# A new order of the scan's operations on the five engines of a hybrid encoder kernel

## What is computed

```
def _wkv_step(S, xs):
    r_t, w_t, k_t, v_t, kk_t, a_t = xs
    sa = jnp.einsum('zbhvk,zbhk->zbhv', S, -kk_t)
    S = (S * w_t[..., None, :]
         + sa[..., :, None] * (kk_t * a_t)[..., None, :]
         + v_t[..., :, None] * k_t[..., None, :])
    o = jnp.einsum('zbhvk,zbhk->zbhv', S, r_t)
    return S, o
...
_, o = lax.scan(_wkv_step, S0, seqs)
```

## Time and profile before

| | us |
|---|---|
| median of 3 runs | 3039.69 (3038.88 to 3043.14) |
| profiled execution, its own time | 3045.98 |
| its span in the trace | 3044.2 |
| scan: unit 0's first matmuls to unit 24's `logits` | 938.00 to 1577.09 |
| scan: from there to the last store | 1577.09 to 1662.21 |
| PE busy in the span | 2655.3 (87%) |
| DVE, ACT, POOL busy | 1410.2, 801.5, 980.1 |

### The profile page before, as it was taken

One profiled execution on the slowest core, in us unless ns is written; L12 is line 12 of the kernel. 1 busy time (PEld: TensorE's weight loads), 2 busy tenths in 40 slices (PEclk: granted clock), 3 DMA queues, 4 the chain that ended last, 5 costly groups with the idle time before them and its releaser, 6 DMA issues. The chain is left out here.

```text
span 3044.2 us, 56483 instructions
## 1 busy us (share of the span) xinstructions
PE 2655.3 (87%) x23399; PEld 2286.7 (75%) x23399; DVE 1410.2 (46%) x2263; ACT 801.5 (26%) x1412; POOL 980.1 (32%) x604
## 2 busy tenths in 40 slices
PE   2599969599995888889986596999999999999996
PEld 1488858455554888888885375999999988999996
DVE  5335435455554565656652695332323263323235
ACT  2212111244442333333331221222122232212211
POOL 3215215346662121211210573332232333323221
PEclk9999989599996899999998698999999999999998
DMA  4222221100002111111111534422212213122211
GB/s 146 68 69 92 67 86 47 58 21 18 8 11 63 49 52 52 55 46 56 49 34 42 181 138 167 128 63 61 69 55 69 62 53 108 55 69 64 60 41 41
DMA packets 210810, 203.48 MB, mean 67 GB/s; under 512 B 16982, under 2 KB 174678, under 8 KB 210618
## 3 DMA queue, kind: packets, MB, share of 16 engines
q1 hardware_dynamic: 210618, 200.67, 21.5%
HBM read 153.45 MB, written 47.18 MB: 66 GB/s over the span
## 5 line engine op out<-in xcount | busy, mean ns | idle before, releaser
L2368 POOL TENSOR_TENSOR ff_w_lo<-ff_w,ff_w_hi 128x1024 fp32r<-128x1024 f32 x132 | 317.4, 2428 | 734.2 <-ACT ff_w_hi L2423 540.0
L2640 PE MATMUL ff_gu<-ff_x_hi,ff_w_hi 128*128 128x384 f32 x1408 | 473.4, 336 | 7.9 <-DVE ff_x_lo L2512 7.9
L2640 PE MATMUL ff_gu<-ff_x_hi,ff_w_lo 128*128 128x384 f32 x1408 | 472.6, 336 | 0.0
L2640 PE MATMUL ff_gu<-ff_x_lo,ff_w_hi 128*128 128x384 f32 x1408 | 472.5, 336 | 0.0
L2521 DVE SCALAR_TENSOR_TENSOR ff_th<-ff_th,ff_gu 128x384 f32<-128x384 f32 x88 | 48.8, 554 | 557.2 <-ACT ff_th L2435 557.2
L2640 PEld LDWEIGHTS ff_gu<-ff_x_hi,ff_w_hi 128*128 128x128 f32 x1408 | 266.0, 189 | 9.3 <-DVE ff_x_lo L2512 8.4
L2640 PEld LDWEIGHTS ff_gu<-ff_x_hi,ff_w_lo 128*128 128x128 f32 x1408 | 266.1, 189 | 0.9
L2640 PEld LDWEIGHTS ff_gu<-ff_x_lo,ff_w_hi 128*128 128x128 f32 x1408 | 265.9, 189 | 0.0
L2534 DVE TENSOR_TENSOR ff_y<-ff_dn,ff_y 128x512 f32<-128x512 f32 x264 | 179.1, 689 | 121.2 <-PE ff_dn L2651 121.0
L2651 PE MATMUL ff_dn<-ff_w_hi,ff_a_hi 128*128 128x512 f32 x528 | 207.1, 392 | 6.9 <-DVE ff_y L2534 6.8
L2651 PE MATMUL ff_dn<-ff_w_hi,ff_a_lo 128*128 128x512 f32 x528 | 206.8, 392 | 0.0
(11 more groups left out here) (273 smaller groups left out, 5269.1 us busy)
## 6 DMA issues: line engine op xcount, KB each, us to landing
ff_w<-in_w_ffn_in SPq DMA_DIRECT2D x88, 512.0 KB, 5.0
ff_w<-in_w_ffn_out SPq DMA_DIRECT2D x44, 512.0 KB, 3.7
sc_x<-scratch_chT SPq DMA_DIRECT2D x72, 256.0 KB, 3.3
pj_x<-in_x SPq DMA_DIRECT2D x13, 512.0 KB, 3.6
co_w<-in_w_in SPq DMA_DIRECT2D x13, 512.0 KB, 5.7
scratch_chT<-co_sh SPq DMA_DIRECT2D x8, 785.0 KB, 4.3
scratch_scan<-sc_out SPq DMA_DIRECT2D x24, 260.0 KB, 2.6
mo_sc<-scratch_scan SPq DMA_DIRECT2D x24, 260.0 KB, 3.0
```

The costliest lines, as they stand in the source:

```text
L2368: nc.gpsimd.tensor_tensor(w_lo[:, q, x, :], w[:, q, x, :], w_hi[:, q, x, :].bitcast(F32), ALU.subtract).then_inc(done, 1)
L2640: last = nc.tensor.matmul(gu[:, g, m, 0:GRP], ww[:, q, m, k * P:(k + 1) * P], xx[:, k, g * GRP:(g + 1) * GRP], start=(j == 0), stop=(j == ...
```

## The change

The three tables that give each operation its place are replaced by other numbers, and the three constants that spaced prep, level and back part (`LEAD`, `LEVEL_SPAN`, `BACK_AT`) are gone, since the new numbers hold the places themselves. No operation is added or removed, and no wait: each operation keeps the semaphores it had.

```
-LEVEL = (("x0", -0.17),) + tuple((f"{x}{l}", (l - 1 + at) / 5) for l in range(1, LEVELS) for x, at in (("y", 0.05), ("mask", 0.25), ("t", 0.5), ("add", 0.75)))
...
-LEAD, LEVEL_SPAN, BACK_AT = 1.4, 1.5, 1.6
...
+LEVEL = (("x0", -0.149), ("y1", -0.0), ("mask1", 0.16), ("t1", 0.221), ("add1", 0.28), ("y2", 0.431), ("mask2", 0.507), ("t2", 0.569), ("add2",
...
+REUSE_AT, VALUES_AT, STORE_AT = -0.73, 2.71, 2.76
...
-    stages = [(u - LEAD + at, 0, "prep", name, u) for u in range(UNITS) for name, at in PREP]
-    stages += [(u + at * LEVEL_SPAN, 1, "level", name, u) for u in range(UNITS) for name, at in LEVEL]
-    stages += [(u + BACK_AT + at, 2, "back", name, u) for u in range(1, UNITS) for name, at in BACK]
-    stages += [(BACK_AT, 3, "meta", "", 0)]
+    stages = [(u + at, 0, "prep", name, u) for u in range(UNITS) for name, at in PREP]
+    stages += [(u + at, 1, "level", name, u) for u in range(UNITS) for name, at in LEVEL]
+    stages += [(u + at, 2, "back", name, u) for u in range(1, UNITS) for name, at in BACK]
+    stages += [(dict(LEVEL)["add5"], 3, "meta", "", 0)]
```

More of the change, by code:

```diff
@@ L1241 @@
 HALF_DECAY = DECAY / 2
-PREP = (("logits", 0.0), ("tanhw", 0.02), ("eye", 0.05), ("tanha", 0.07), ("cum", 0.1), ("gate", 0.12), ("lift", 0.14),
[3 rows of a table removed]
-LEVEL = (("x0", -0.17),) + tuple((f"{x}{l}", (l - 1 + at) / 5) for l in range(1, LEVELS) for x, at in (("y", 0.05), ("mask", 0.25), ("t", 0.5), ("add", 0.75)))
-BACK = (("drive", 0.02), ("carry0", 0.05), ("U1_0", 0.1), ("solve0", 0.16), ("U0", 0.21), ("state0", 0.28), ("H0", 0.34),
-        ("carry1", 0.48), ("U1_1", 0.55), ("solve1", 0.61), ("U1", 0.66), ("state1", 0.73), ("H1", 0.79), ("emit", 0.87), ("out", 0.95))
+PREP = (("logits", -1.328), ("tanha", -1.264), ("tanhw", -1.241), ("gate", -1.218), ("lift", -1.179), ("kd", -1.128), ("cum", -1.112), ("rkd",
[3 rows of a table added]
+LEVEL = (("x0", -0.149), ("y1", -0.0), ("mask1", 0.16), ("t1", 0.221), ("add1", 0.28), ("y2", 0.431), ("mask2", 0.507), ("t2", 0.569), ("add2",
+         0.621), ("y3", 0.724), ("mask3", 0.776), ("t3", 0.936), ("add3", 0.988), ("y4", 1.049), ("mask4", 1.101), ("t4", 1.157), ("add4", 1.209),
+         ("y5", 1.312), ("mask5", 1.494), ("t5", 1.526), ("add5", 1.586))
+BACK = (("drive", 1.773), ("carry0", 1.855), ("U1_0", 1.904), ("solve0", 1.985), ("U0", 2.013), ("state0", 2.098), ("H0", 2.13), ("carry1", 2.273),
+        ("U1_1", 2.322), ("solve1", 2.361), ("U1", 2.389), ("state1", 2.621), ("emit", 2.647), ("out", 2.691), ("H1", 2.798))
 RING = 4
-LEAD, LEVEL_SPAN, BACK_AT = 1.4, 1.5, 1.6
+REUSE_AT, VALUES_AT, STORE_AT = -0.73, 2.71, 2.76
 UNITS = 2 * STEPS + 1
@@ L1470, in store @@
                     sp.dma_start(d["scan"][un.s, un.tile * P:(un.tile + 1) * P, :], out[:, un.ring, :]).then_inc(out_stored[un.ring], 16)
-                moves = [(un.u - 2 - LEAD + 0.47, load, un) for un in units[1:]]
-                moves += [(un.u - RING + BACK_AT + 1, load_values, un) for un in units[1:]]
-                moves += [(un.u + BACK_AT + 1, store, un) for un in units[1:]]
+                moves = [(un.u - 2 + REUSE_AT, load, un) for un in units[1:]]
+                moves += [(un.u - RING + VALUES_AT, load_values, un) for un in units[1:]]
+                moves += [(un.u + STORE_AT, store, un) for un in units[1:]]
                 for _, move, un in sorted(moves, key=lambda x: x[0]):
```

## The result

The changed kernel takes 2951.15 us (median, 2946.34 to 2953.66), against 3041.41 for the kernel before in the same series: a ratio of 0.970, 95% interval 0.969 to 0.971. The forecast was 2953 in a range of 2936 to 2994. The profiled execution took 2953.66 with a span of 2951.9, so 92.3 us less than the span of before.

A forecast was written before the change was run, and what follows sets the result against it. PE bounds the scan, losing time to queueing waits at `state0` and `y3` and to clock dips. Savings of 68.4 (steady), 9 (fill) and 9 us (drain) take 3045.98 to 2959.6; the median, 6.3 lower, is 2953 us, range 2936 to 2994.

## What to carry to other kernels

When an engine's wait ends with an operation that started at the heels of another, the queue is the cause; moving one operation is worth trying, but walk on to what stood behind the moved one, since `state0` alone brought 10 us and three new waits. Take a period's own work from a period that has all the work in it (compare instruction counts), and once an engine is busy throughout, look at which matmul shapes alternate: here that gave another 0.5%.

## What the runs showed of the hardware

**Long waits and short ones differ for the clock, but not by a fixed length.** In before, `state0`'s wait is by turns 2.06 and 1.65 us, and the clock falls to 1.2 GHz behind 15 of the 18; without the other wait it falls behind 8 of 14. With `state0` late there are four short waits in every period, 1.06, 0.81, 0.89 and 0.4 us, and PE is idle for longer. The windows view of that kernel:

```profile
1110.00:1480.00 370.00, 326.77 (x7394) 298.12 (x7390) 251.08 (x415) 142.84 (x308) 74.46 (x56) 1.00 0.19 54
```

PE is idle for 12% of that stretch and the clock stays at 1.00; with the copies late it is idle for 7% and the clock is 0.96. So in these windows the fall goes with the long waits, and not with the idle time as a whole. It is no rule. Behind that window the kernel with `state0` late has one fall, at 1526.82, in a period whose waits are 1.06, 0.81, 0.76 and 0.89 us:

```profile
1511.62:1540.16 28.54, 25.03 (x534) 22.83 (x532) 18.32 (x31) 10.30 (x23) 5.39 (x4) 0.94 0.18 50
```

And in the changed kernel's fill the clock falls at 996.53 among waits of 0.78, 0.96, 0.85 and 1.05 that stand within 7 us. The Trainium skill (TensorE: Matmul & The Clock Gate, A second HAM failure mode) has micro-idles between groups of matmuls that make the clock oscillate; here, in the kernels whose periods have no longer waits than 1.07 us, the clock fell in that one and in no other of their 18 periods. Why some waits bring a fall and others of the same length don't stays open.

**Neighbours change what a matmul costs**, by 0.3 us at each of two places, as above, and a busy PE is no sign that nothing waits: `y4` starts just behind its X in a stretch that shows no idle time.

**DVE and POOL stop each other.** `tK` was 0.69 us on DVE when it began 0.05 us ahead of POOL's decay of H, which then took 1.54; beginning 0.29 behind it, POOL keeps 1.04 and `tK` takes 1.30. Lines view, 1100 to 1460, of before and then of after (xcount | busy us, mean ns):

```profile
L1652 DVE TENSOR_TENSOR sc_KRT<-sc_x,sc_Wd 128x512 f32<-128x512 f32 x13 | 9.0, 693 | 0.4
```

```profile
L1654 DVE TENSOR_TENSOR sc_KRT<-sc_x,sc_Wd 128x512 f32<-128x512 f32 x16 | 20.7, 1296 | 0.0
```

With the gate late, `tC` beside `rkd` takes 1.75 and ends 0.54 behind it (rows above), `tK` ends 0.55 behind the decay. The Trainium skill (SBUF — State Buffer, Who interferes with whom) says that a DVE operation with both inputs in SBUF contends with POOL's reads and that whoever starts first makes the other wait; these rows agree. DVE has the room for it here, since no wait of PE ends with it; the prediction has no term for it.
